# Expert rows summed by TensorE's diagonal products, and the gathers in the order context, latent, context

## What is computed

```python
def peer_ffn(h, wq, subkeys, u, v):          # per token: 8 heads x 16 experts = 128 rows of u and of v
    scores = einsum('bthpd,hpkd->bthpk', qr, subkeys)
    s1, i1 = top_k(scores[..., 0, :], 16); s2, i2 = top_k(scores[..., 1, :], 16)
    top, pos = top_k(cand, 16)               # of the 16 x 16 sums
    gate = softmax(top)
    act = gelu(einsum('ted,td->te', u[ek], hk))
    return einsum('te,ted->td', gk * act, v[ek])
for l in range(DEPTH):                        # first block
    hc = modulate(rms_norm(xc, norm1_g[l]), sh1c, sc1c)
    if l < DEPTH - 1:                         # context: mixer, then experts
        yc, s_f, s_b = token_mixer(hc, ...)
        xc = xc + g2c * peer_ffn(...)
    else:                                     # context: final states only
        s_f, s_b = hgrn2_final_states(iv_c, zf_c, zb_c, lbf, lbb)
    yx, _, _ = token_mixer(hx, ..., s_f, s_b, latent_conv)
    x = x + g2x * peer_ffn(hx2, ...)
```

## Time and profile before

| | us |
|---|---|
| median of three runs | 4341.35 |
| the profiled execution | 4339.68 |
| its span, first to last instruction | 4337.8 |
| TensorE busy | 1973.4 (45%) |
| VectorE busy | 3194.8 (74%) |
| ScalarE busy | 708.9 (16%) |
| GpSimd busy | 934.8 (22%) |
| DMA, mean over the span | 1150.09 MB, 265 GB/s |

### The profile page before, as it was taken

How to read it: one execution, slowest core, us unless ns; L and a number is a source line. 1 busy time by engine, 2 the same in 40 slices (tenths; PEclk the granted TensorE clock), 3 DMA queues, 4 the chain that set the end, 5 groups by cost and what they waited for, 6 DMA issues and landing times.

```text
span 4337.8 us, 29160 instructions
## 1 busy us (share of the span) xinstructions
PE 1973.4 (45%) x9362; PEld 1353.8 (31%) x9362; DVE 3194.8 (74%) x5528; ACT 708.9 (16%) x1125; POOL 934.8 (22%) x803
## 2 busy tenths in 40 slices
PE   7787111208754121110418642121230476977688
PEld 1676000006633000000318530000110344947386
DVE  0464899998976999999886569999878753546354
ACT  0312000001110000001112110000100242523053
POOL 0000333332222333333320013333334100000000
PEclk9898555658877555555759876555565687978789
DMA  7324899998887899999963269898999512533054
GB/s 262 136 83 154 343 362 351 354 382 331 323 321 275 346 365 368 360 367 358 373 248 122 104 235 376 354 360 337 358 365 363 209 68 94 188 126 132 14 189 146
DMA packets 275597, 1150.09 MB, mean 265 GB/s; under 512 B 19466, under 2 KB 19573, under 8 KB 176720
## 3 DMA queue, kind: packets, MB, share of 16 engines
q0 software_dynamic: 113264, 814.26, 47.7%
q1 hardware_dynamic: 162016, 334.19, 21.3%
q10 hardware_dynamic: 192, 0.20, 0.0%
HBM read 1147.33 MB, written 1.25 MB: 265 GB/s over the span
## 4 chain that ended last, share of the span: by engine, by line
DVE 42%; PE 27%; DMA 18%; issue 10%; ACT 2%; SPq 0%; POOL 0%; POOLq 0%; DVEq 0%; ACTq 0%
DVE arena L1631 15%; DMA arena<-in_peer_uv,arena 13%; DVE arena L1609 8%; PE ps L631 5%; PE ps L633 5%; PE ps L632 5%; PE ps L616 4%; DVE w_lo L1297 2%; DMA vec<-mods 1%; PE ps L705 1%; DVE arena L1403 1%; DVE arena L1526 1%; DVE arena L1529 1%; DVE arena L1535 1%; PE ps L625 1%
## 5 line engine op out<-in xcount | busy, mean ns | idle before, releaser
L1897 POOL DMA_INDIRECT arena<-in_peer_uv,arena x768 | 916.2, 1193 | 2321.3 <-DVE arena L1631 1547.2
L1631 DVE SCALAR_TENSOR_TENSOR arena<-arena 128x1024 f32<-128x1024 f32 x762 | 977.8, 1283 | 13.6
L705 PE MATMUL ps<-ring,condS 128*2 128x512 f32 x768 | 400.6, 684 | 1266.7 <-DVE mod_io L1673 1239.5
L1609 DVE CUSTOM_DVE_ANT_0 arena<-arena,hA 128x1024 f32<-128x1024 f32 x512 | 625.1, 1221 | 91.3 <-DMA arena<-in_peer_uv,arena 86.7
L705 PEld LDWEIGHTS ps<-ring,condS 128*2 128x2 f32 x768 | 67.7, 92 | 1596.3 <-DVE mod_io L1673 1278.3
L1297 DVE TENSOR_TENSOR w_lo<-ring,w_hi 128x1024 fp32r<-128x1024 f32 x272 | 326.1, 1223 | 216.6 <-ACT w_hi L996 209.9
L1120 ACT ACTIVATE arena<-arena 128x2 f32<-128x2 f32 x384 | 78.1, 203 | 2259.4 <-DVE arena L1609 2259.2
L631 PE MATMUL ps<-hT_hi,w_hi 128*128 128x256 f32 x1408 | 407.8, 290 | 44.1 <-DVE hT_lo L1305 38.3
L632 PE MATMUL ps<-hT_lo,w_hi 128*128 128x256 f32 x1408 | 404.8, 287 | 0.0
L633 PE MATMUL ps<-hT_hi,w_lo 128*128 128x256 f32 x1408 | 404.4, 287 | 0.0
L1609 DVE CUSTOM_DVE_ANT_0 arena<-arena,hB 128x1024 f32<-128x1024 f32 x256 | 312.6, 1221 | 46.5 <-DMA arena<-in_peer_uv,arena 43.9
(11 more groups left out here) (266 smaller groups left out, 2955.0 us busy)
## 6 DMA issues: line engine op xcount, KB each, us to landing
ring<-in_w_mod SPq DMA_DIRECT2D x48, 2048.0 KB
ring<-in_w_in SPq DMA_DIRECT2D x64, 512.0 KB, 6.4
ring<-in_w_mlp_in SPq DMA_DIRECT2D x64, 512.0 KB, 5.9
ring<-in_w_mlp_out SPq DMA_DIRECT2D x64, 512.0 KB, 5.6
ring<-in_w_in SPq DMA_DIRECT2D x11, 2048.0 KB
ring<-in_peer_wq SPq DMA_DIRECT2D x32, 512.0 KB, 7.9
vec<-mods SPq DMA_DIRECT2D x31, 512.0 KB, 7.7
ring<-in_w_out SPq DMA_DIRECT2D x6, 2048.0 KB
```

Of the source, the lines that this page charges most:

```text
L705: mm = pe.matmul(o, condS[:, k, 2 * (l // 2):2 * (l // 2) + 2], ring[:, s, k, :], start=k == 0, stop=k == KT - 1)
L1609: dve.tensor_tensor_reduce(row, row, peer_buf[p][:, t, :], 1.0, 0.0, ALU.mult, ALU.add, dots[:, col:col + 1]).then_inc(dot_done, 1)
L1631: ins = dve.scalar_tensor_tensor(acc, row, c, acc, ALU.mult, ALU.add)
L1897: pool.indirect_dma_start(uv[:, j % SLOTS, :], None, A["peer_uv"], at).then_inc(uv_full[j % SLOTS], 16)
```

## The change

**Rows on TensorE.** `add_row` leaves VectorE. `weigh` now writes, for each row, the diagonal matrix `ident * coef * gate` (128x128, one `tensor_scalar` with two scalar columns) over the used u row in the slot. TensorE multiplies it with the v row, two float32 matmuls of 512 columns, and accumulates a tile's sum in PSUM banks 6 and 7. GpSimd waits for `pe_added`. `flush` reads the sum from PSUM.

**Order of the gathers.** 384 pairs of rows are numbered through. Seven segments: p = 0 tile 0, the first quarter of p = 0 tile 1, both tiles of p = 1, the other three quarters of p = 0 tile 1, and both tiles of p = 2. In layer 0 the context's last 96 selections thus come after the latent's. The scores of the late quarters are stored in DRAM (`held`) and loaded again.

**Timetable.** Instead of a rate, each piece on each engine has a slot number, that of the pair before which it must have been issued. `weave(first, last, ...)` issues a pair's work first and then every piece that is due, stream by stream. Pairs 0 to 255 carry: 4 picks (slots 0 to 11), norm, mixer 1 (projection pieces of a quarter chunk at 7 to 10 and 13 to 29, levels at 17 to 32, tail 33 to 37), its output projection (38 to 41), norm and queries (43 to 59), scores, 8 picks (61 to 100), modulation 1 (84 to 107) and 2 (108 to 131), 3 picks (104 to 118), the filters (136 to 154), the norm of the latent in layer 1 (208), and the whole front of mixer 3 (projection 213 to 233, levels 221 to 236). Levels use two PSUM banks and are split by direction: 16 steps of 8 matmuls instead of 9 of 16. Pairs 256 to 383 carry 7 picks, modulation 3 (292 to 315), and keys and values (322 to 347).

**What stays without gathers** between pairs 255 and 256: the context's norm, mixer 2 (three chunks, with split operands), the states, the output of mixer 3, its projection, and the queries of p = 2. Mixer 3's projection uses plain float32 operands; its convolution is kept in `HV`.

**Lead-in.** Three small constants come first, so modulation 0 starts before the big ones; masks are bytes. Chunks 0 to 7 of modulation 0 stand before mixer 0, 8 and 9 inside it, 10 and 11 in the first gathers; the norm's parts lie between them. Mixer 0 makes the states after its output projection.

**Filters.** Their tables are loaded by SP after the picks of p = 0; the two spectra are stored in DRAM (`spectra`) and loaded as `Kf` after the first feed-forward network. One barrier goes.

```diff
-        RATE = (3, 5), (1, 2), (3, 5)
-        def weave(p, rate, segment, *stages):
-            pieces = (x for stage in stages for x in stage)
-            more, due = True, 0
-            for g in range(ALLGRP + 1):
-                segment(p, g)
-                due += rate[0]
-                while more and due >= rate[1]:
-                    due -= rate[1]
-                    more = next(pieces, pieces) is not pieces
-            run(pieces)
+        def weave(first, last, segment, *streams):
+            due = [next(x, None) for x in streams]
+            for g in range(first, last + 1):
+                segment(g, first, last)
+                for n, x in enumerate(streams):
+                    while due[n] is not None and due[n] <= g:
+                        due[n] = next(x, None)
@@ timetable
+        SEGS = [(0, 0, 0, NSEL), (0, 1, 0, NQ), (1, 0, 0, NSEL), (1, 1, 0, NSEL), (0, 1, NQ, NSEL),
+                (2, 0, 0, NSEL), (2, 1, 0, NSEL)]
+                self.level = [r + 4 + i for i in range(16)]
+        TIMES = {1: Times(2, 7, 2), 3: Times(PAIRS[3], PAIRS[3] + 5, 0)}
+        OUT, POST, WQ, SCORES = 38, 43, 48, 60
+        MOD_AT = {1: 84, 2: 108, 3: FIRST_PAIRS + 36}
+        FILTERS = 136
+        KV = FIRST_PAIRS + 66
@@ TensorE
+            def add_row(j):
+                pe.wait_ge(diag_ready, pe_upto[j + 1])
+                if start and seg:
+                    pe.wait_ge(sums_taken, seg)
+                for c in range(2):
+                    mm = pe.matmul(ps[:, 6 + c, :], uv[:, j % SLOTS, 0:P], uv[:, j % SLOTS, D + c * CW:D + (c + 1) * CW],
+                                   start=start, stop=stop)
+                mm.then_inc(pe_added, 1)
+            def segment(g, first, last):
+                if g > first:
+                    for j in (2 * g - 2, 2 * g - 1):
+                        if on_pe(j):
+                            add_row(j)
+            weave(0, FIRST_PAIRS, segment,
+                  itertools.chain(early_mods(), turn_norm_pieces("n_x0", TIMES[1].turn), front_pieces(1)), level_pieces(1),
+                  itertools.chain(back_pieces(1), turn_norm_pieces("p_x0", POST + 3), query_pieces(1), score_pieces(1),
+                                  modulation(1), modulation(2), filters(),
+                                  turn_norm_pieces("n_x1", TIMES[3].turn), front_pieces(3)), level_pieces(3))
@@ VectorE
-                    ins = dve.scalar_tensor_tensor(acc, row, c, acc, ALU.mult, ALU.add)
-                ins.then_inc(axpy_done, 1)
+            def weigh(j):
+                dve.wait_ge(gelu_done, j // 2 + 1)
+                if on_pe(j):
+                    dve.tensor_scalar(uv[:, j % SLOTS, 0:P], ident[:, :], c, gate, ALU.mult, ALU.mult).then_inc(diag_ready, 1)
+            def segment(g, first, last):
+                done = (2 * g - 2, 2 * g - 1) if g > first else ()
+                for s in range(2):
+                    if g < last:
+                        dot(2 * g + s)
+                    if s == 0:
+                        for j in done:
+                            weigh(j)
+                if done and 2 * g in SEG_END:
+                    flush(SEG_END.index(2 * g))
@@ VectorE, one level step per slot
+                    elif i == 15:
+                        crossings(base + 16)
+                    else:
+                        lev, d = (i - 1) // 2, (i - 1) % 2
+                        dve.wait_ge(lev_mm, base + i + 1)
+                        st.do(put_level(d, lev, 0, 4))
+                        ins = put_level(d, lev, 1, 5)
+                        if d == 0:
+                            ins.then_inc(lev_ready, 1)
+                        else:
+                            st.do(ins)
+                            scan_update(lev, True, lambda ins: ins.then_inc(lev_ready, 1))
@@ GpSimd
-                pool.wait_ge(axpy_done, j + 1)
+                k = j - SLOTS
+                if k >= 0 and on_pe(k):
+                    pool.wait_ge(pe_added, pe_upto[k + 1])
```

More of the change, by code:

```diff
@@ L1190, in _, with early_mods @@
-            run(norm_pieces("n_x1"), mixer(3), norm_pieces("p_x1"), peer_queries(2), peer_part(2, 0))
-            weave(2, RATE[2], segment, blend(peer_parts(2), modulation(3)), norm_pieces("n_kv"), kv_pieces())
+            def early_mods():
+                for c in range(10, 12):
+                    yield c - 8
+                    modulation0(c, c + 1)
+            modulation0(0, 4)
+            root(0)
+            modulation0(4, 6)
+            split_high(L_in[0], 0)
+            modulation0(6, 8)
@@ L1520, in top16, with back_pieces @@
+            def back_pieces(m):
+                yield TIMES[m].tail + 4
+                weigh_out(m, 1)
+                for c in range(2):
+                    yield OUT + 2 * c + 2
+                    gated_chunk("r_x0", L_out[m], c, hB)
+                residual("r_x0", L_out[m], xs, hB)
             def top16(values, index, source, rows_):
@@ L1634, in group @@
[L1634 to L1655 removed]
+                ins.then_inc(dve_added, 1)
@@ new lines, in _ @@
+            squares(cs, 0, hA)
+            modulation0(4, 6)
+            inverse(0)
+            norm_scale("n_c0", cs)
+            norm_shift("n_c0")
+            modulation0(6, 8)
+            turn_parts("n_c0")
+            mixer0()
+            norm("p_c0", cs)
+            queries(0)
+            run(pick((0, 0, 0)))
+            weave(0, FIRST_PAIRS, segment, pick_pieces(PICK_ORDER[1:5]), early_mods(),
+                  norm_pieces("n_x0", xs, TIMES[1].norm), front_pieces(1),
+                  itertools.chain(back_pieces(1), norm_pieces("p_x0", xs, POST)),
+                  pick_pieces(PICK_ORDER[5:16]),
+                  itertools.chain(modulation(1), modulation(2), filter_pieces(), norm_pieces("n_x1", xs, TIMES[3].norm)),
+                  front_pieces(3))
@@ new lines, in _ @@
+            norm("n_c1", cs)
+            L = L_in[2]
+            for d in range(2):
+                forget(2, d)
+            for lev in range(LEVELS):
+                if lev < LEVELS - 1:
+                    scan_update(lev, False, st.do)
+                    st.settle()
+                else:
+                    scan_update(lev, False, lambda ins: ins.then_inc(scan_ready, 1))
+            weigh_out(3, 2)
+            gated("r_x1", L_out[3], xs, hA)
+            norm("p_x1", xs)
+            queries(2)
@@ L1693, in _ @@
+            run(pick((2, 0, 0)))
+            weave(FIRST_PAIRS, ALL_PAIRS, segment, pick_pieces(PICK_ORDER[17:]), modulation(3), context_pieces())
             rms(xs, 0, hA)
```

1322 lines of the change are left out of this document (826 added, 496 removed).

## The result

The changed kernel takes 4564.4 us, the median of four runs (4560.15 to 4567.23), against 4341.7 for the kernel before on the same chip (4330.94 to 4344.67). The ratio is 1.0517, with an interval of 1.0497 to 1.0537: 5.2% slower. The forecast was 4482 us with a range of 4230 to 4620. The sign and the range held, and the sum was 82 us short.

A forecast was written before the change was run, and what follows sets the result against it. VectorE and DMA were both taken as near their limits in the first gathers. 4337.8 - 62 + 306 - 72 + 19 - 50 = 4479; the runs' median lies 3.5 us above: forecast 4482 us, range 4230 to 4620.

The forecast's parts named there:

- the level slot: Slots 17 to 32 and 221 to 236: VectorE waits for TensorE's rows, quarter and level product; 222 us each.
- B: The stretch of the first 512 gathers: 2113 us against 1807, +306; bounds 1951 to 2168.
- Bare slots: Pairs of gathers with little else to do, slots 155 to 207: 5.6 us each, 297 us.
- Pick slots and filters: First 512 gathers: picks in slots 63 to 83 at 6.3 us, 132 us; filters in slots 132 to 154, 143 us.
- The floor of a pair: DMA time for two gathers: 5.33 us, from 393.5 GB/s; 5.5 us at the best share, 0.97.
- Rival 2: DMA paces everything, VectorE's slack fills the pipeline: first 512 gathers 1750 us, total 4077 us; chance 0.15.
- Stage D: The last 256 gathers: 858 us against 839, +19; bounds 820 to 900.
- Lead-in: Before the gathers: fewer chunks before the first norm, first split product at about 80; -62 us, bounds -45 to -70.
- Gap: Between first and last gathers: only three split chunks stay; -72 us, bounds -60 to -80.
- Filters' end: Filters standing alone, 59 us, go; 9 us charged for loads losing their cover; -50 us.
- Rival 1: The levels don't chain: a level slot costs TensorE's 8.8 us, first 512 gathers 1951, total 4320 us; chance 0.19.
- Rival 3: TensorE stays at the lower clock, its rows pacing bare and pick slots: +250, 4730 us; chance 0.08.

The follow-up runs named there:

- the last kernels: Diagonals ahead of the first dot, level product ahead of the rows, and rows shared between TensorE and VectorE by slot, redrawn, against the kernel before: 4138.94 us, ratio 0.9532.
- the last run: One extra VectorE product after the first dot of each bare slot, added to the kernel with level product and diagonals first, all rows on TensorE: 4222.05 us.

## Why the prediction was right, and where it was not

**The sign and its mechanism: right, and shown.** The step that carried the slower forecast was the level slot with TensorE in the middle of it. It was put at 13.3 us plus 1.25 for the clock with a quarter and 13.9 on average; it measured 14.6 and 14.7 (+26 us in the two stretches). Undoing only that place in the queue gave 188 us. That TensorE would be the next to be late was right in the sense of order, not of load: it is busy 1695 of 2189 us in B, 195 above the 1500 of the sum, and the same instructions fit into 4229 us.

**Bare slots: mis-sized, and the reason was missed.** Put at 5.6, measured 6.03 (B, +23 us) and 6.1 (D). The prediction had the rows land 2 us later and charged 0.1. It didn't follow the diagonals one step back: they stand behind a dot that waits for its own landing, so that each release waits for a later transfer. The kernel with the diagonals first shows the missing 0.6 to 1.0 us.

**Pick slots and filters: mis-sized.** Picks of slots 63 to 83 were put at 6.3 and took 7.3 (+22), filters at 6.2 and 7.4 (+27). Of the 49 us, 22 go with the diagonals' place; the remaining 27 were not isolated. The two terms were too low for either engine: with all rows on VectorE the same slots took 8.4 and 7.2. Modulation slots were put at 8.5 and took 8.1 (-19), less than the 8.23 of DMA in the forecast. All other lines of B lay within 5 us, but for the first 13 slots (+7, and 6 before them) and the pairs after the second levels (-10): together +76, the whole miss of B, which ends above its bound of 2168.

**The floor of a pair: wrong as a floor.** 5.33 us came from the gather queue's bytes over its share of the time. That is a mean cost under the conditions of that kernel, and it was read as a bound. Bare slots of D took 5.04, at 410 GB/s (the kernel with the diagonals first, 3288 to 3479 us). Rival 2's estimate, 1750 us for B, was therefore no lower bound either, though no kernel reached it.

**Stage D: +39 for +19.** The stretch took 882 where 858 was forecast. Its bare slots account for most of it: 38 of them at 6.1, where 5.6 would have been 18 us less. Same cause as above. The picks (233 us for 220) and modulation (190 for 204) cancel, and the start of the stretch took some 9 us more than its 10.

**Lead-in: -51 for -62.** The chain of the changed kernel:

```profile
44.28 7.04 PE ps L812 x16
51.34 11.85 DMA ring<-in_w_mod
63.24 16.35 PE ps L812 x32
...
87.32 0.55 PE ps L718
```

The first split product came at 87.3, put at 80: from one chunk at 44.28 to the next but one at 63.24 it is 19.0 us with a load of 11.85 between them, where the forecast took 15.2 for two chunks. The last two, after that wait, took 16.35 us, and 13.94 in the kernel before. The other 3 us lie behind the first split product and were not followed.

**Gap: -83 for -72.** Here a row was misread. The 36.6 us of the earlier trace rows that the first two chunks were charged are the time of three, as ScalarE's evictions in the kernel before show:

```profile
2276.18 1.02 ACT L1042 ACTIVATE arena<-ps 128x1024 f32<-128x1024 f32 x1 [12.52 <-PE ps L633]
...
2287.70 1.03 ACT L1042 ACTIVATE arena<-ps 128x1024 f32<-128x1024 f32 x1 [1.81 <-PE ps L633]
...
2299.22 1.02 ACT L983 ACTIVATE arena<-ps 128x1024 f32<-128x1024 f32 x1 [1.00 <-PE ps L633]
```

The first two end after 25 us there, and in the changed kernel too (from the first split product at 2590.35 to 2615.28). The 11.6 us charged too much are the miss, and they put the gap outside its bounds of -60 to -80.

**Filters' end: -53 for -50.** The cover that was lost shows as predicted, a load of rows on the chain where there was none:

```profile
4139.83 8.16 DMA vec<-mods
...
4161.83 0.58 PE ps L718
```

It lasts 8.2 us, but the norm's first steps run beside it. Before, it was 18.0 us from the end of the filters (3918.02) to the next split product (3936.04); now it is 22.9 from the end of the network (4138.9) to 4161.83. So the lost cover cost 4.9 us of the 9 charged.

**The rivals.** Rival 1 was false for the changed kernel and true of a kernel with the product first: 8.5 us a slot. Rival 2 came nearest in the last kernels, 4139 us against its 4077. Rival 3 had the clock fall in bare slots; it stood at 0.91 there, and at 0.83 in the levels.

## What to carry over

When work moves to an engine that stands in the middle of another chain, its size says little: count what is queued behind it on that engine and who waits for that, and issue first what another engine waits for. The same holds on the engine that prepares the operand: an instruction that waits for a transfer must not stand ahead of one that releases a transfer. Then share the moved work by stretch, and price whole stretches, as a slot's gain may be its neighbour's loss.

## What the hardware showed

A queue's bytes over its busy share gave 393.5 GB/s, and later kernels moved 402 and 414 at shares of 1.00 and 1.01: the rate at nearly the same busy share differed from kernel to kernel (381 GB/s at 0.98 with rows on VectorE, 371 at 0.98 with every other row). VectorE's load alone is not the reason, at least up to the 155 of 190 us of the last run; what it is stays open. The Trainium skill (DMA: Bandwidth & Descriptors, section Specifications) gives about 358 GB/s of HBM for a core, half of a stack's 716. This program runs on one core, and its trace does not show that limit: 414 over 191 us.

One row after 3 us of idling cost more than two rows without it (3.78 us against 3.60), so halving the rows of a level slot shortened it by a tenth only.
